# Two transformer blocks on one core: one weight group and spread modulation loads for one-stream feed-forwards, waits by halves for two streams, and matmuls of constants around the transposes

## The chip, the cores and the metric

The kernel runs on one core of a Trainium2 chip. The metric is the device time of one execution in microseconds (us), as the median of several runs. The core has TensorE (PE, matrix multiply), VectorE (DVE), ScalarE (ACT), GpSimd (POOL), and SyncE (SP), whose queue issues nearly all DMAs. They run their own instruction streams and meet only at semaphores.

## What is computed

Two blocks in float32 on 256 tokens of width 1024. Block 1 has two layers; each is feed-forward, mixer, feed-forward, and works on two streams, the tokens `x` and a context of the same size. The mixer of layer 0 is a gated MLP (gMLP), that of layer 1 is attention. After that attention only `x` goes on. Block 2 has two layers of feed-forward, mixer ("mix": attention, convolution and gated linear attention side by side), feed-forward, on `x` alone.

```python
def ffn_sublayer(x, shift, scale, gate, w_in, w_out, ln_g, ln_b):          # block 1
    y = swiglu(modulate(x, shift, scale), w_in, w_out)
    return layer_norm(ALPHA * x + 0.5 * gate * y, ln_g, ln_b)

for l in range(DEPTH):                                                      # block 2
    mod = c_act @ ada_w[l] + ada_b[l]
    sh1, sc1, gt1, sh2, sc2, gt2, sh3, sc3, gt3 = jnp.split(mod, N_MOD, axis=-1)
    h = _modulate(_rmsnorm(x, ffn1_norm[l]), sh1, sc1)
    x = x + FFN_RES * gt1[:, None, :] * _swiglu(h, ffn1_w_in[l], ffn1_w_out[l])
    ...                                                                     # mixer, second feed-forward
```

`swiglu(h, w_in, w_out)` is `(silu(h @ w_g) * (h @ w_u)) @ w_out` with an inner width of 2816, that is 22 chunks of 128. Every sublayer has its own shift, scale and gate vectors (three sections of 1024), each a product of a condition vector with a 1024 x 1024 matrix.

## The kernel before

**Stages.** `plan()` lists twelve stages, here called by their number: 0 feed-forward, 1 gMLP, 2 and 3 feed-forward, 4 attention (its input has two streams, its output one), 5 feed-forward, all block 1; 6 feed-forward, 7 mix, 8 and 9 feed-forward, 10 mix, 11 feed-forward, all block 2. Stages 0 to 4 have two streams (512 columns a matmul), 5 to 11 one (256). The feed-forwards with one stream are 5, 6, 8, 9 and 11.

**Units.** The weights come in units of 1 MB (two DMAs) through two slots of `wraw`. Each unit is split into a high part `wh` (ACT, L697) and a low part `wl` (DVE, L1023, function `split_next`), and every product is three matmuls (L1656). SP may load unit u when `wl` of unit u-2 is made (L428). ACT makes `wh` of a unit only when PE is through with the unit two before it (L696), and PE starts a unit when its `wl` is there.

**A feed-forward** goes in two groups, `GROUPS = (12, 10)` chunks of the inner width. For each group there is a features phase (one unit a chunk: gate and up products into the PSUM banks 0,1 or 2,3, then ACT's silu L758, DVE's product `ht` L1245, POOL's split into `hh` and `hl` L557, L558) and an out phase (one unit for two chunks, L1779). The y tiles of an out phase, 128 tokens by 1024, take two banks each: banks 0 to 7 with two streams, 4 to 7 with one. After each group `take_y` (DVE, L1114 and L1117) adds the gated tiles to `x`, and adds 1 to `y_evac` when the last tile has left PSUM. PE waits for `y_evac` before a group's features with two streams (L1838), and for `pair_free`, the last `ht`, before every out phase (L1841). In stages whose input isn't scaled yet, DVE multiplies and adds the layer norm's gain and bias to `x` after the features of the first group (`scale_x`, L1249, instructions of L1137), ahead of the split of the second out unit.

**The modulation of the next stage** is made during the features phase of the first group: 12 DMAs of 1 MB (`mraw`, L421) and for each of them two DVE operations a stream (`mod_unit`, L1000). Three sections of four pieces q go by turns of four units. `mods_taken` (L351) says that the first unit of a turn takes pieces 0 and 1, the second piece 2, the third piece 3. `mods_loaded` (L354) issues pieces 0 and 1 at unit 1 of SP's turn and 2 and 3 at unit 3. At a section's end PE turns the row into columns (`columns`, L1665) and DVE copies them (`mod_end`).

**Between two stages** PE runs `gate_rows` (L1676, f32 matmuls of `ones` with `acc` after `y_evac`), then `transposes` (L1696, 16 a stream, f32, `ident` moving) after the norm of the stage, which DVE, ACT and POOL make; ACT and DVE evacuate and split the transposed input (L728, L1083, L736, L1075), and then the next features start (L1710, or L1750 in mix and attention).

Of the kernel before, what the change touches and what calls it, by code (L numbers as in the profile page):

```python
# [6 lines left out]
P = 128  # L7
# [10 lines left out]
T = 256  # L18
# [4 lines left out]
GROUPS = (12, 10)  # L23
# [17 lines left out]
CW = 256  # L41

# [9 lines left out]
def plan():  # L52
# [14 lines left out]
    n = dict(unit=FIRST, inq=FIRST, h=FIRST, sg=0, group=0, pre=0, tr=0, mix=0, tile=0)  # L67
    for i, s in enumerate(subs):
# [6 lines left out]
        if s["kind"] == "ffn":  # L75
            n["unit"] += KF + KF // 2
# [3 lines left out]
            n["group"] += len(GROUPS)  # L80
            n["tile"] += len(GROUPS) * (TT * ns - 1)
        elif s["kind"] == "gmlp":
# [4 lines left out]
            n["group"] += 2  # L87
            n["tile"] += 2 * (TT * ns - 1)
# [68 lines left out]
def program(nc, ins, out, subs):  # L157
    u_end = subs[-1]["n_unit"] + dict(ffn=33, gmlp=36, attn=10, mix=16)[subs[-1]["kind"]]
    with ExitStack() as ctx:
# [76 lines left out]
        zt = (zt0, zt1)  # L236

# [62 lines left out]
        y_evac = sem("y_evac")  # L300
# [50 lines left out]
        def mods_taken(per, j, i):  # L351
            return [(i, q) for q in ((0, 1), (2,), (3,), ())[j]] if per == 4 else [(j // 2, 2 * (j % 2) + q) for q in (0, 1)]

        def mods_loaded(per, j, i):  # L354
            if per == 4:
                return [(i, q) for q in ((), (0, 1), (), (2, 3))[j]]
            n = j - 2 if j else 0
            return [] if j in (1, 2) else mods_taken(per, n, i)

        def section_done(per, j, i):  # L360

            sec = (i if j == per - 1 else None) if per == 4 else (j // 2 if j % 2 else None)
# [46 lines left out]
        def _(sp):  # L409
# [66 lines left out]
            for s in subs:  # L476
                nxt = after(s)
                if s["kind"] == "ffn":
# [4 lines left out]
                    for g, n in enumerate(GROUPS):  # L483

                        phase(n, 2 if g else 4, lambda idx: [
# [54 lines left out]
        def _(pool):  # L540
# [69 lines left out]
            for s in subs:  # L610
# [15 lines left out]
                if s["kind"] == "ffn":  # L626
                    m0 = 0
                    for g, n in enumerate(GROUPS):
# [59 lines left out]
        def _(act):  # L688
# [50 lines left out]
            for s in subs:  # L739
# [7 lines left out]
                if s["kind"] == "ffn":  # L747
                    W = T * len(s["streams"])
                    m0, u0 = 0, s["n_unit"]
                    for g, n in enumerate(GROUPS):  # L750
# [224 lines left out]
        def _(dve):  # L975
# [122 lines left out]
            def take_y(s, streams, bank0, u, first, tiles=None, by=zt):  # L1098
# [5 lines left out]
                for i in range(n):  # L1104
# [9 lines left out]
                    steps.link(dve.tensor_tensor(by[t][:], ps[:, b:b + 2].rearrange("p a b -> p (a b)"), gate[:, c], ALU.mult))  # L1114
                    if i == n - 1:
# [108 lines left out]
            for s in subs:  # L1224
# [8 lines left out]
                if s["kind"] == "ffn":  # L1233
                    W = T * len(s["streams"])
                    m0, u0 = 0, s["n_unit"]
                    for g, n in enumerate(GROUPS):
# [10 lines left out]
                        phase(n, u0, 2 if g else 4, evac, None if g else nxt)  # L1247
# [8 lines left out]
                        take_y(s, s["post"], 0 if W == 2 * T else 4, u0, g == 0, s["n_tile"] + g * (W // P - 1),  # L1256
                               zt if g else zm)
# [397 lines left out]
        def _(pe):  # L1655
# [23 lines left out]

            def transposes(s):  # L1680
# [86 lines left out]
            def out_unit(u, count, width, bank0, chunk0, ready, start=False, stop=False, halves=None):  # L1767
# [4 lines left out]
                for t in range(width // P):  # L1772
# [437 lines left out]
```

## Time and profile before

| | us |
|---|---|
| median of 3 runs | 3416.32 (3415.41 to 3417.49) |
| the profiled execution | 3414.92, of which the span of the trace is 3413.2 |
| PE busy / DVE busy / ACT busy / POOL busy in the span | 3116.1 / 2017.1 / 969.2 / 651.2 |
| TensorE clock granted, mean | 0.954 of full speed |
| DMA, mean | 153 GB/s |

All rows are of one execution. PEclk 1.00 is 2.4 GHz and 0.50 is 1.2 GHz. Matmuls overlap, so that the last of a run ends 0.2 to 0.4 us after its slot; the distance between starts is the rate. "DVEq" or "issue" as the end of a wait is an instruction of a queue (a semaphore) or one that the trace doesn't show.

### The profile page before, as it was taken

The page shows a single profiled execution, that of the slowest core. Times are in us where ns is not written, and L with a number is a line of the kernel's source. Part 1 is how long each engine was busy: PE and PEld are TensorE (multiplying, and loading weights), DVE is VectorE, ACT ScalarE, POOL GpSimd, SP SyncE. Part 2 cuts the span into 40 slices and gives each one's busy share as a digit, 9 for nine tenths or more (in the row PEclk, how much of TensorE's full clock was granted, in tenths as well). Part 3 has the DMA queues.
Part 4 walks back from the last instruction along what each step waited for, and adds up shares of the span by engine and source line. Part 5 has one row for each costly group of instructions (what it writes and reads, how often), then busy time and mean ns, then how long its engine had stood idle before and what let it go on. Part 6 is the DMA issues. An engine that isn't in the chain of part 4 may idle for free.

```text
span 3413.2 us, 45375 instructions
## 1 busy us (share of the span) xinstructions
PE 3116.1 (91%) x17444; PEld 2660.2 (78%) x17444; DVE 2017.1 (59%) x1834; ACT 969.2 (28%) x981; POOL 651.2 (19%) x628
## 2 busy tenths in 40 slices
PE   7999989999989999899988799799888989989799
PEld 3877779877768787777867689688877878978688
DVE  6653366656276434773348775664687557457654
ACT  1111222212122121211214333333533333343333
POOL 0110100214011010110100031122552103227011
PEclk9999989999989999899999899899889989989899
DMA  7533235222254333443333686675447658654355
GB/s 274 163 124 89 95 112 173 99 87 75 87 155 152 100 86 111 136 136 99 98 102 124 202 269 182 202 229 179 171 148 239 208 176 281 189 172 151 120 178 159
DMA packets 501022, 523.00 MB, mean 153 GB/s; under 512 B 15652, under 2 KB 432726, under 8 KB 500886
## 3 DMA queue, kind: packets, MB, share of 16 engines
q1 hardware_dynamic: 497720, 513.76, 46.8%
q0 software_dynamic: 3168, 7.36, 1.0%
q8 instruction: 96, 1.57, 0.2%
q14 instruction: 38, 0.31, 0.0%
HBM read 520.01 MB, written 1.05 MB: 153 GB/s over the span
## 4 chain that ended last, share of the span: by engine, by line
PE 70%; DVE 15%; issue 5%; DMA 4%; ACT 3%; POOL 2%; SPq 1%; DVEq 0%; ACTq 0%; POOLq 0%
PE ps L1710 37%; PE ps L1779 19%; PE ps L1750 7%; DMA mraw<-in_ada_w 3%; DVE wl L1023 3%; DVE acc L1000 2%; DVE x L1117 2%; ACT wh L697 2%; DVE x L1137 1%; PE ps L1696 1%; PE ps L1665 1%; DVE zt L1114 1%; POOL wst L667 1%; DVE mraw L1114 1%; ACT ptmp L728 1%
## 5 line engine op out<-in xcount | busy, mean ns | idle before, releaser
L1023 DVE TENSOR_TENSOR wl<-wraw,wh 128x2048 fp32r<-128x2048 f32 x341 | 846.9, 2484 | 681.6 <-ACT wh L697 672.7
L1710 PE MATMUL ps<-xh,wh 128*128 128x256 f32 (+1 forms) x3008 | 1003.4, 334 | 68.0 <-DVE xl L1075 38.2
L1710 PE MATMUL ps<-xh,wl 128*128 128x256 f32 (+1 forms) x3008 | 996.0, 331 | 0.0
L1710 PE MATMUL ps<-xl,wh 128*128 128x256 f32 (+1 forms) x3008 | 995.0, 331 | 0.0
L697 ACT ACTIVATE wh<-wraw 128x2048 fp32r<-128x2048 f32 x341 | 652.3, 1913 | 655.5 <-PE ps L1779 622.5
L1710 PEld LDWEIGHTS ps<-xh,wh 128*128 128x128 f32 x3008 | 574.7, 191 | 135.3 <-issue 65.0
L1710 PEld LDWEIGHTS ps<-xl,wh 128*128 128x128 f32 x3008 | 573.7, 191 | 58.8
L1710 PEld LDWEIGHTS ps<-xh,wl 128*128 128x128 f32 x3008 | 574.6, 191 | 57.5
L1000 DVE SCALAR_TENSOR_TENSOR acc<-mraw,svec,acc 128x1024 f32<-128x1024 f32 x329 | 431.6, 1335 | 44.4 <-DMA mraw<-in_ada_w 29.9
L557 POOL CAST hh<-ht 128x256 f32 (+1 forms) x176 | 135.7, 771 | 1578.3 <-DVE ht L1245 1578.3
L1779 PE MATMUL ps<-wh,hh 128*128 128x512 f32 x968 | 386.6, 399 | 25.5 <-DVE ht L1245 19.8
L1779 PE MATMUL ps<-wl,hh 128*128 128x512 f32 x968 | 384.9, 398 | 0.0
L1779 PE MATMUL ps<-wh,hl 128*128 128x512 f32 x968 | 384.5, 397 | 0.0
L758 ACT ACTIVATE sg<-ps 128x256 f32<-128x256 f32 (+1 forms) x176 | 81.8, 465 | 983.7 <-PE ps L1710 983.7
L1245 DVE TENSOR_TENSOR ht<-ps,sg 128x256 f32<-128x256 f32 (+1 forms) x176 | 92.0, 523 | 380.2 <-ACT sg L758 379.7
L1750 PE MATMUL ps<-wh,xh 128*128 128x256 f32 x896 | 265.0, 296 | 37.2 <-DVE wl L1023 19.1
L1750 PE MATMUL ps<-wl,xh 128*128 128x256 f32 x896 | 261.3, 292 | 0.0
L1750 PE MATMUL ps<-wh,xl 128*128 128x256 f32 x896 | 260.7, 291 | 0.0
L1779 PEld LDWEIGHTS ps<-wh,hh 128*128 128x128 f32 x968 | 182.9, 189 | 74.9 <-DVE ht L1245 24.4
L1779 PEld LDWEIGHTS ps<-wh,hl 128*128 128x128 f32 x968 | 183.1, 189 | 44.4
L1779 PEld LDWEIGHTS ps<-wl,hh 128*128 128x128 f32 x968 | 182.9, 189 | 43.7
L1750 PEld LDWEIGHTS ps<-wh,xh 128*128 128x128 f32 x896 | 179.2, 200 | 41.6 <-DVE wl L1023 21.9
(332 smaller groups left out, 2981.2 us busy)
## 6 DMA issues: line engine op xcount, KB each, us to landing
wraw<-in_ffn_w_in SPq DMA_DIRECT2D x352, 512.0 KB, 5.1
wraw<-in_ffn_w_out SPq DMA_DIRECT2D x176, 512.0 KB, 4.2
mraw<-in_ada_w SPq DMA_DIRECT2D x72, 1024.0 KB, 7.4
mraw<-in_w_mod SPq DMA_DIRECT2D x64, 1024.0 KB, 5.7
wraw<-in_gmlp_w_in SPq DMA_DIRECT2D x48, 512.0 KB, 4.5
wraw<-in_mix_w_in SPq DMA_DIRECT2D x48, 512.0 KB, 4.6
wraw<-in_gmlp_w_out SPq DMA_DIRECT2D x24, 512.0 KB, 4.3
first_w<-in_w_mod SPq DMA_DIRECT2D x8, 1024.0 KB, 13.4
```

The source lines that it names most:

```text
L557: steps.link(pool.tensor_copy(hh[:, where], ht[:, par, 0:width]))
L667: op = pool.tensor_scalar(term, ch_t[:, 1, tap:tap + T], cw_t[:, 1, tap:tap + 1], cw_t[:, 1, CONV_K:CONV_K + 1] if tap == 0 else None, ALU ...
L697: act.activation(wh[:, slot], wraw[:, slot], ACT.Copy).then_inc(whi_done, 1)
L758: act.activation(sg[:, pair, 0:W], ps[:, 2 * pair, 0:W], ACT.Silu).then_inc(sg_ready, 1)
L1000: op = dve.scalar_tensor_tensor(out=acc[:, c], in0=mraw[:, q % 2, jj], scalar=svec[:, v, 2 * q + jj:2 * q + jj + 1], in1=biasrow[:] if q = ...
L1023: dve.tensor_tensor(wl[:, slot], wraw[:, slot], wh[:, slot].bitcast(F32), ALU.subtract)\
L1114: steps.link(dve.tensor_tensor(by[t][:], ps[:, b:b + 2].rearrange("p a b -> p (a b)"), gate[:, c], ALU.mult))
L1117: last = steps.mark(dve.scalar_tensor_tensor(out=x[:, c, t], in0=x[:, c, t], scalar=ALPHA if first and s["block"] == 1 else 1.0, in1=by[t] ...
L1245: dve.tensor_tensor(ht[:, pair, 0:W], ps[:, 2 * pair + 1, 0:W], sg[:, pair, 0:W], ALU.mult)\
L1710: m = pe.matmul(ps[:, bank, 0:width], a, b, start=k == p == 0, stop=k == KD - 1 and p == 2)
L1750: m = pe.matmul(to, a, b, start=k == p == 0, stop=k == KD - 1 and p == 2)
L1779: m = pe.matmul(ps[:, bank0 + 2 * t + half], a, b, start=start and kk == p == 0, stop=stop and kk == 1 and p == 2, skip_group_check=not st ...
```

## The change

The feed-forwards with one stream have one group of 22 chunks, whose y tiles are taken once, with the unused second halves of `gate` and `acc` as temporaries. Their modulation goes by turns of eight units, one piece at a time; the last six units (two turns of eight fit in 22) take the four pieces of the last section by lists of their own. The out phase no longer waits for `pair_free` with one stream. With two streams and in the gMLP, `take_y` adds 1 to a new semaphore `y_half` after its second tile, on which the features phase (banks 0 to 3) now waits; the first out unit writes the tiles of banks 4 to 7 first and waits for `pair_free` before the others (in the gMLP the order stays, and the wait moves to the third tile). In all feed-forwards the split of the second out unit comes ahead of `scale_x`. In the gMLP DVE's order is as it was. `keep_going(bank, 16)` issues 16 f32 matmuls of `ones` with `ident`, 128 columns each, into a bank that nobody reads: ahead of the transposes of stages 1 to 11, and behind the transposes of stages 5 to 11.

```diff
-GROUPS = (12, 10)
+GROUPS = {2: (12, 10), 1: (22,)}
+LAST_TAKEN, LAST_LOADED = (0, 1, 3, 5), (0, 2, 4, 5)
...
+        by_one = (gate[:, 1], acc[:, 1])
...
         def mods_taken(per, j, i):
+            if per == 8:
+                at = LAST_TAKEN if isinstance(i, int) and i == 2 else (0, 2, 4, 6)
+                return [(i, q) for q in range(4) if at[q] == j]
...
         def mods_loaded(per, j, i):
+            if per == 8:
+                at = LAST_LOADED if isinstance(i, int) and i == 2 else (1, 3, 5, 7)
+                return [(i, q) for q in range(4) if at[q] == j]
...
@@ take_y
+                    if i == TT - 1 < n - 1:
+                        dve.sem_inc(y_half, 1)
...
@@ DVE, feed-forward
-                        phase(n, u0, 2 if g else 4, evac, None if g else nxt)
+                        phase(n, u0, 2 if g else 8 if one else 4, evac, None if g else nxt)
+                        split_next(u0 + n)
                         if g == 0:
                             scale_x(s, s["post"])
...
-                        phase(n // 2, u0 + n, 2)
+                        phase(n // 2 - 1, u0 + n + 1, 2)
...
@@ PE
+            def keep_going(bank, n):
+
+                for _ in range(n):
+                    pe.matmul(ps[:, bank, 0:P], ones[:], ident[:], start=True, stop=True)
...
-                for t in range(width // P):
+                for n, t in enumerate(late[0] if late else range(width // P)):
+                    if late and n == TT:
+                        late[1]()
...
                 gate_rows(s)
+                if s["i"]:
+                    keep_going(3, 16)
                 transposes(s)
+                if len(s["post"]) == 1 and len(s["streams"]) == 1:
+                    keep_going(7, 16)
...
-                            pe.wait_ge(y_evac, s["n_group"] + g)
-                        features_phase(n, u0, s["n_inq"] + m0, W, 2 if g else 4, None if g else nxt)
-
-                        pe.wait_ge(pair_free, s["n_inq"] + m0 + n + 1)
+                            pe.wait_ge(y_half, s["n_half"] + g)
+                        features_phase(n, u0, s["n_inq"] + m0, W, 2 if g else 4 if both else 8, None if g else nxt)
+
                         pe.wait_ge(y_evac, s["n_group"] + g)
...
-                                  lambda i: pe.wait_ge(h_ready, s["n_h"] + m0 + 2 * i + 3))
+                                  lambda i: pe.wait_ge(h_ready, s["n_h"] + m0 + 2 * i + 3),
+                                  late=((2, 3, 0, 1), lambda: pe.wait_ge(pair_free, s["n_inq"] + m0 + n + 1)) if both else None)
...
@@ PE, gMLP
-                        pe.wait_ge(y_evac, s["n_group"] + g)
+                        pe.wait_ge(y_half, s["n_half"] + g)
...
+                            if i == first:
+                                pe.wait_ge(y_evac, s["n_group"] + g)
...
-                        pe.wait_ge(pair_free, q1 + first + n + 1)
+                        pe.wait_ge(sg_ready, s["n_sg"] + 2 * (first + n))
...
+                                  late=((0, 1, 2, 3), lambda: pe.wait_ge(pair_free, q1 + first + n + 1)))
```

## Rows read from the trace of the kernel before

**Rows 1.** The page: busy time of each engine; the chain of waits by engine.

```profile
PE 3116.1 (91%) x17444; PEld 2660.2 (78%) x17444; DVE 2017.1 (59%) x1834; ACT 969.2 (28%) x981; POOL 651.2 (19%) x628
...
PE 70%; DVE 15%; issue 5%; DMA 4%; ACT 3%; POOL 2%; SPq 1%; DVEq 0%; ACTq 0%; POOLq 0%
```

**Rows 2.** PE's waits over the span: line, releaser, us in total, times, longest.

```profile
PE ps L1710 <- DVE xl L1075: 38.2, 8, 5.0
PE ps L1696 <- issue: 34.9, 6, 13.8
PE ps L1676 <- DVEq L1116: 31.5, 11, 7.8
...
PE ps L1710 <- DVE wl L1023: 21.2, 24, 2.0
PE ps L1779 <- DVE ht L1245: 19.8, 16, 1.6
...
PE ps L1710 <- DVEq L1116: 8.6, 4, 2.3
PE ps L1779 <- DVE wl L1023: 8.0, 5, 2.0
...
PE ps L1779 <- DVEq L1310: 7.3, 2, 3.7
```

**Rows 3.** The chain, first out phase of stage 8: start, us, what.

```profile
2668.21 28.27 PE ps L1779 x120
```

**Rows 4.** The chain, first out unit of stage 2: start, us, what.

```profile
1112.31 6.06 DVE x L1137 x4
...
1118.39 4.64 DVE x L1137 x4
...
1123.34 2.30 DVE wl L1023
...
1125.69 2.62 PE ps L1779 x7
```

**Rows 5.** The page's group of `mod_unit`: busy, mean ns | idle before.

```profile
L1000 DVE SCALAR_TENSOR_TENSOR acc<-mraw,svec,acc 128x1024 f32<-128x1024 f32 x329 | 431.6, 1335 | 44.4 <-DMA mraw<-in_ada_w 29.9
```

**Rows 6.** Stretches of stage 8: features of first and second group; busy, clock, DMA share, GB/s.

```profile
2590.00:2667.00 77.00, 73.66 (x606) 72.85 (x605) 64.62 (x50) 24.96 (x23) 27.19 (x21) 0.97 0.90 287
...
2703.00:2758.00 55.00, 54.38 (x466) 54.13 (x465) 29.32 (x22) 21.18 (x19) 10.23 (x18) 1.00 0.65 188
```

**Rows 7.** PE's timeline from stage 8's end into stage 9: start, us [idle before].

```profile
2791.20 2.69 PE L1676 MATMUL ps<-acc,ones 128*128 128x512 f32 x4 [2.77 <-DVEq L1116]
2797.28 3.65 PE L1696 MATMUL ps<-ident,z 128*128 128x128 f32 x16 [3.39 <-issue]
2805.65 0.58 PE L1710 MATMUL ps<-xh,wh 128*128 128x256 f32 x1 [4.72 <-DVE xl L1075]
```

**Rows 8.** Short stretches at the starts of stages 9 and 8; columns as in rows 6.

```profile
2788.90:2792.20 3.30, 0.99 (x3) 0.55 (x4) 3.15 (x3) 0.00 (x0) 0.00 (x0) 1.00 1.01 393
2792.30:2795.70 3.40, 1.59 (x3) 0.03 (x1) 0.42 (x3) 2.19 (x4) 0.72 (x1) 0.50 1.05 275
...
2580.70:2584.00 3.30, 3.30 (x16) 3.21 (x16) 0.00 (x0) 0.00 (x0) 0.00 (x0) 0.50 0.00 0
2584.10:2587.40 3.30, 0.16 (x2) 0.00 (x0) 1.90 (x4) 3.07 (x6) 0.00 (x0) 1.00 0.00 0
```

**Rows 9.** First features of stages 5 and 11, at 0.50 of the clock; columns as before.

```profile
1945.50:1949.10 3.60, 3.60 (x17) 3.60 (x18) 3.00 (x3) 2.49 (x2) 0.00 (x0) 0.50 0.00 0
...
3215.00:3218.90 3.90, 3.90 (x18) 3.90 (x19) 3.69 (x3) 1.04 (x1) 0.00 (x0) 0.50 0.02 4
```

**Rows 10.** PE's timeline in the gMLP: f32 matmuls of 128 columns at full clock.

```profile
641.73 0.38 PE L1877 MATMUL ps<-wst,ones 128*128 128x128 f32 x2
...
642.17 1.95 PE L1881 MATMUL ps<-wst,v 128*128 128x128 f32 x16
```

**Rows 11.** PE's timeline at the start of stage 1: transposes at full clock.

```profile
467.13 1.97 PE L1696 MATMUL ps<-ident,x 128*128 128x128 f32 x16 [1.32 <-DVEq L1159]
```

More of the change, by code:

```diff
@@ L65, in plan @@
             subs.append(dict(block=2, layer=l, kind=kind, part=part, streams=(0,), post=(0,)))
-    n = dict(unit=FIRST, inq=FIRST, h=FIRST, sg=0, group=0, pre=0, tr=0, mix=0, tile=0)
+    n = dict(unit=FIRST, inq=FIRST, h=FIRST, sg=0, group=0, half=0, pre=0, tr=0, mix=0, tile=0)
     for i, s in enumerate(subs):
@@ L75, in plan @@
         if s["kind"] == "ffn":
+            s["groups"] = GROUPS[ns]
             n["unit"] += KF + KF // 2
@@ L79, in plan @@
             n["sg"] += KF
-            n["group"] += len(GROUPS)
-            n["tile"] += len(GROUPS) * (TT * ns - 1)
+            n["group"] += len(s["groups"])
+            n["half"] += len(s["groups"]) if ns == 2 else 0
+            n["tile"] += len(s["groups"]) * (TT * ns - 1)
         elif s["kind"] == "gmlp":
@@ L87, in plan @@
             n["group"] += 2
+            n["half"] += 2
             n["tile"] += 2 * (TT * ns - 1)
@@ L482, in _ @@
                     m0 = 0
-                    for g, n in enumerate(GROUPS):
-                        phase(n, 2 if g else 4, lambda idx: [
+                    for g, n in enumerate(s["groups"]):
+                        phase(n, 2 if g else 4 if len(s["streams"]) == 2 else 8, lambda idx: [
                             w_in[:, :, t, bass.ds(idx + m0, 1), :].rearrange("p k m c -> p k (m c)")
@@ L627, in _ @@
                     m0 = 0
-                    for g, n in enumerate(GROUPS):
+                    for g, n in enumerate(s["groups"]):
                         pool.wait_ge(w_used, s["n_unit"] + 18 * g)
@@ L749, in _ @@
                     m0, u0 = 0, s["n_unit"]
-                    for g, n in enumerate(GROUPS):
+                    for g, n in enumerate(s["groups"]):
                         q0 = s["n_inq"] + m0
@@ L1235, in _ @@
                     m0, u0 = 0, s["n_unit"]
-                    for g, n in enumerate(GROUPS):
+                    one = len(s["groups"]) == 1
+                    for g, n in enumerate(s["groups"]):
                         q0, h0 = s["n_inq"] + m0, s["n_h"] + m0
@@ L1253, in _ @@
                             factors(nxt)
-                        phase(n // 2, u0 + n, 2)
+                        phase(n // 2 - 1, u0 + n + 1, 2)
                         u0 += n + n // 2
-                        take_y(s, s["post"], 0 if W == 2 * T else 4, u0, g == 0, s["n_tile"] + g * (W // P - 1),
-                               zt if g else zm)
+                        take_y(s, s["post"], 4 if one else 0, u0, g == 0, s["n_tile"] + g * (W // P - 1),
+                               by_one if one else zt if g else zm)
                         m0 += n
@@ L1765, in all_tokens_phase, with out_unit @@
                 mod_loop(pe, n, per, body, mods)
-            def out_unit(u, count, width, bank0, chunk0, ready, start=False, stop=False, halves=None):
+            def out_unit(u, count, width, bank0, chunk0, ready, start=False, stop=False, halves=None, late=None):
                 slot = u % 2
@@ L1783, in out_unit, with out_phase @@
                 m.then_inc(w_used, 1)
-            def out_phase(n, u0, width, bank0, ready, halves=None):
+            def out_phase(n, u0, width, bank0, ready, halves=None, late=None):
                 for i in range(n):
-                    out_unit(u0 + i, u0 + i, width, bank0, 2 * i, lambda: ready(i), i == 0, i == n - 1, halves)
+                    out_unit(u0 + i, u0 + i, width, bank0, 2 * i, lambda: ready(i), i == 0, i == n - 1, halves,
+                             None if i else late)
             def input_halves(chunk, t):
```

8 lines of the change are left out of this document (4 added, 4 removed).

## The prediction, as it went on record

> **What bounds the kernel now.** I read the page first: PE is busy for 91% of the span and holds 70% of the chain [rows 1]. So only three things count: time in which PE waits, time in which it works at half clock, and work put on it. The view of PE's waits sorts the first kind [rows 2]. The stretches of the trace with their granted clock give the second, and PE's timeline at the stage boundaries shows how much room there is for added matmuls; both are taken up below. All terms below are differences in PE's time, since next to nothing else is late at the end.
>
> **Waits that the finer order removes.**
> Start of an out phase: PE waits 19.8 us in all, 16 times, for the last `ht` [rows 2]. That is every group of the feed-forwards: six with two streams (about 1.5 each), ten with one (about 1.1). With one stream the y banks 4 to 7 are apart from the banks 0 to 3 that `ht` reads, and no wait is left. With two streams the first two tiles take banks 4 to 7: 24 matmuls at 0.236 us [rows 3] are 5.7 us of work ahead of a wait that would have been over in 1.5. The low half of the first out unit is made before the last `ht` in either order, so nothing else is late there. **19.8 off.** Five of these sixteen phase starts no longer exist at all, which comes to the same.
> Start of the second group's features with two streams, and in the gMLP: 8.6 us, four times, for the last of four tiles [rows 2]. `y_half` comes two tiles, so about 5 us, earlier, ahead of PE's end of the out phase. **8.6 off.**
> Start of an out phase in the gMLP: 7.3 us, twice [rows 2]. The new wait, for ACT's `sg`, is over before the gating matmuls end, and half an out unit (5.7 us) covers the 3.7. But in the first group DVE still does 12 us of `scale_x` before the second out unit's split, and PE waits for that already now; there the second unit starts when it did, and the gain is given back. **3.7 off, of 7.3.**
> `scale_x` [rows 4]: in stage 2 it takes 10.7 us, then `wl` 2.3, and the second out unit starts 13.4 us after the last `ht`, where the first out unit (48 matmuls) is 11.4 long: 1.9 lost, in stage 3 the same. With the split first, the 10.7 us lie beside two out units (22.4 us) with the next split: 1.9 off in each. In stage 5 it takes 5.3 (four of those eight operations) and an out unit 5.6: counted from the end of the features, `wl` of the second out unit is ready at 5.0, `scale_x` ends at 10.3, the next `wl` at 12.6, where PE wants it at 11.2. So 1.4 of the 2.0 come back one unit later. **4.4 off**, out of the 8.0 of five waits [rows 2]; the other two are not touched.
>
> **One group with one stream, modulation by eight.** PE waits 21.2 us, 24 times, for `wl` in the features phases [rows 2], all of them in feed-forwards with one stream, nearly all in the first groups of stages 5, 6, 8 and 9, where the modulation is made, the rest behind `take_y`. Why: a unit of features is 48 matmuls at 55 us / 466 [rows 6], so a split has to be ready 5.6 us after the one before it. In a turn's first unit DVE does two pieces, four operations of 1.3 us [rows 5], beside 2.3 for the split and 0.4 for `ht`: 8 us of work in 5.6. In the first group DVE is busy for 64.6 of 77 us and DMA for 0.90 of the time; in the second for 29.3 of 55 and 0.65 [rows 6]. Spread over 22 units (about 124 us): DVE 22 x 3.0 and the difference of 29, so 95 us or 0.77. DMA 0.65 x 5.6 = 3.64 us a unit; twelve units are 43.7 of the 69.3 seen, which leaves 25.6 us for the modulation; so 80.1 + 25.6 = 105.7 in 127, or 0.83, and 0.85 to 0.92 in the last six units, which take four pieces. A unit with one piece fits: split done at 5.0 us, piece at 7.6, `ht` at 8.0, and the next `wh` is not there before 8.3. SP issues a piece two units, some 11 us, before it is used. What could be left is lateness of DMA in the last six units, from 0 to 17. I keep 1 us a stage. **17 off.** The pieces moved on SP's queue go behind each weight unit's pair, so a unit's weights queue behind at most one piece, not two. The `take_y` that disappears is DVE time that PE only feels as part of these waits: nothing more.
>
> **The matmuls of constants, price.** An f32 matmul is two PE instructions in the trace (x2 for one call), and 16 of 128 columns take 1.95 us with 0.28 of tail: 0.111 us each [rows 10]. So a block of 16 is 32 x 0.111 = 3.6 us at full clock. Transposes in f32 take 1.97 for 16 at full clock [rows 11] and 3.65 at half [rows 7]; by their distances the block is 32 x 0.215 = 6.9 us at half clock. Eighteen blocks are 65 to 124 us, so it matters where they lie.
> Ahead of the transposes of stages 7 to 11, PE sits idle for 3.4 us in stage 9 [rows 7], up to 5.5 in the mixes; these waits and the longer one of stage 6 are the 34.9 us of [rows 2]. `gate_rows` in front of it took 2.7 us, part of it at half clock. So at full clock 3.6 us go in with about 0.5 to spare. Behind the transposes PE is idle for 4.7 us [rows 7], one of the eight waits of 38.2 us in all [rows 2]: 3.6 goes in with 1.1 to spare, 6.9 would be 2.2 late.
> With two streams (stages 1 to 4) the block delays the first stream's transposes by 0.5 to 4 us, but DVE is busy with the second stream's norm meanwhile and comes to them some 3.8 us later. Nothing; between 2 us of gain and 6 of loss for the four.
>
> **What the clock gives back.** In stage 9 the clock was full while PE did the last out unit and was idle for 2.8 us, and fell to half in the next stretch [rows 8]; it came back only in the features. All seven one-stream stages begin their features at 1.2 GHz, for 3.6 to 5.6 us, 29.9 in all (the first and the last are [rows 9]). At 2.4 GHz that work is half as long: 14.9. A run of 16 transposes at half clock was followed by full clock (from 2580.70 and from 2584.10) [rows 8], and they stream `ident`, as the new matmuls do, at the same 0.215 us; so I take it that these raise and hold it. The idle 2.8 us ahead of `gate_rows` stay, so it will often still fall once there and come back under the first block, which then ends up to 1 us late. I take nine tenths: **13.4 off**. The transposes of stages 7 to 11 run at full clock, 3.65 - 1.97 = 1.7 us less each, minus 0.6 each for the late block: **5.4 off**. In stages 5 and 6 the norm between is long or DVE late; transposes there stay at half clock and only the second block helps.
>
> The Trainium skill, "TensorE: Matmul & The Clock Gate", Part 4 (PE-mode transpose), says that the full clock doesn't engage for transposes, as they don't count as busy. The row disagrees: full clock followed right behind 3.6 us of nothing but transposes [rows 8].
>
> **Sum.** 19.8 + 8.6 + 3.7 + 4.4 + 17 + 13.4 + 5.4 = 72.3 us off the profiled execution's 3414.9, so 3342.6. The median of the runs is 1.4 above that execution: **3344.0**.
>
> **Rivals.**
> (a) The clock is held at only half of the boundaries, because the fall comes later than I think, between the blocks: half of 18.8 lost, 3353.4. For it: the idle time in front of `gate_rows` is unchanged. 0.13.
> (b) DMA is the next bound in the one-group phase: the 17 don't come, 3361. For it: 0.85 to 0.92 near the end of the phase, and 0.90 is where stalls are seen now [rows 6]; against it: DMA reached 393 GB/s between stages [rows 8], and 287 in the stalling phase. 0.10.
> (c) The two-stream waits are taken over by the next one (a split behind `take_y` or `scale_x`): half of 19.8 + 8.6 + 3.7 + 4.4, 3362. Against it: splits have 11.2 us a unit there. 0.03.
> (d) Transposes don't count for the clock: stages 5 and 6, where they come first after idle time, start their features at half clock and with the second block 2.2 us late: about 4.5 each, 3353. This is what the skill's Part 4 would make of it. 0.03.
> (e) The blocks never raise the clock, and run at half clock. Then they are late by 4.5 in stages 8, 9 and 11, 3.1 in the mixes, 4.2 in stage 5, 2.3 behind seven sets of transposes, 0.7 with two streams: 43. Only 53.5 - 43 = 10 off, 3406. 0.05.
> (f) **Slower:** the blocks lie on the path in full at half clock, 18 x 6.9 = 124 us against 53.5: 3487. That needs PE to come to them when the norm is already there, and it decides at 53.5 / 18 = 3.0 us a block. Against it: 3.4 and 4.7 us of measured idle time at both places [rows 7]. 0.04.
> My forecast has the remaining 0.62. Its own range is 3330 to 3355; with (a) to (d) 3328 to 3370, which leaves out (e), (f) and some of the tails. Within 0.2% (7 us, about what a measurement of this kernel can tell from no change) needs a mixture of (e) and (b): 0.01. Slower 0.04, faster 0.95.
>
> **What the profile after would show.** PE's waits for `ht` (L1245) ahead of the out phase gone, the waits for L1116 only ahead of `gate_rows`, those for `wl` in features a few us instead of 21; DVE's idle time for `mraw` small and, if (b), in the last six units. Mean clock up from 0.954 to about 0.965. The first 3.6 us of features in stages 5 to 11 at 1.00; if (a) or (e), 0.50. Transposes of 1.97 instead of 3.65 in stages 7 to 11. The forecast is wrong if the blocks' 32 instructions take far more than 3.6 us, if they end after the norm by more than a microsecond, or if `wl` is still late in the phase of 22 units.

## The result and the profile after

The changed kernel took **3322.4 us** (median of four runs, 3317.3 to 3327.0) beside 3415.9 for the kernel before in the same job; the ratio is 0.9728, 95% interval 0.9711 to 0.9745. A second set of five runs gave 0.9724 (0.9711 to 0.9738). The forecast of 3344 had the sign, and the mechanisms that it named were at work, but the time lies 6 us below the low end of its range. The profiled execution took 3321.9 with a span of 3320.1, so 93.1 us less than the 3413.2 before, where 72.3 had been forecast. Some 21 us of gain were not foreseen, and they are what the experiments are about.

The page of the changed kernel, busy time and the chain by engine (answers to [rows 1]):

```profile
PE 3137.9 (95%) x18020; PEld 2698.3 (81%) x18020; DVE 1988.0 (60%) x1814; ACT 972.5 (29%) x985; POOL 635.6 (19%) x628
...
PE 80%; DVE 10%; ACT 3%; POOL 3%; issue 2%; DMA 2%; SPq 0%; DVEq 0%; ACTq 0%; POOLq 0%
```

PE works longer than before (3137.9 against 3116.1), with the 18 x 32 = 576 instructions of the blocks in it, and still ends 93 us earlier.

PE's waits in the changed kernel (line, releaser: us in total, times, longest), to be held against [rows 2]:

```profile
PE ps L1691 <- DVEq L1129: 31.5, 11, 8.0
...
PE ps L1730 <- DVE xl L1086: 19.7, 8, 4.9
...
PE ps L1716 <- issue: 14.3, 5, 9.2
...
PE ps L1801 <- DVE wl L1034: 10.4, 4, 7.2
...
PE ps L1730 <- DVE wl L1034: 3.4, 7, 0.6
```

The lines have moved: L1691 is `gate_rows`, L1716 the transposes, L1730 the features, L1801 the out phase. The wait of the out phase for `ht` (19.8), that of the features for the y tiles (8.6) and that of the gMLP's out phases (7.3) have no row any more. The features' wait for `wl` fell from 21.2 to 3.4. The wait for `xl` ahead of the features and the one ahead of the transposes, 38.2 and 34.9 before, are halved, since the blocks lie in them. One row grew by more than 0.2 us: the out phase's wait for `wl`, from 8.0 to 10.4.

PE's timeline from stage 8's end into stage 9 (against [rows 7]):

```profile
2720.04 1.96 PE L1691 MATMUL ps<-acc,ones 128*128 128x512 f32 x4 [2.47 <-DVEq L1129]
2721.83 3.73 PE L1698 MATMUL ps<-ident,ones 128*128 128x128 f32 x32
2726.12 1.94 PE L1716 MATMUL ps<-ident,z 128*128 128x128 f32 x16 [0.56 <-issue]
2727.90 3.74 PE L1698 MATMUL ps<-ident,ones 128*128 128x128 f32 x32
2732.78 0.38 PE L1730 MATMUL ps<-xh,wh 128*128 128x256 f32 x1 [1.15 <-DVE xl L1086]
```

A block takes the forecast 3.6 us and its tail, and leaves 0.56 us ahead of the transposes and 1.15 behind them (0.5 and 1.1 were forecast). The transposes take 1.94 instead of 3.65. From `gate_rows` to the first feature it is 12.74 us, 14.45 before.

First features of stages 5 and 11 (against [rows 9]), and then two stretches of stage 8's one phase of 22 units (against [rows 6]): busy time, clock, DMA share, GB/s:

```profile
1909.90:1913.50 3.60, 3.57 (x30) 3.58 (x31) 3.00 (x3) 2.53 (x2) 0.00 (x0) 1.00 0.02 5
...
3127.90:3131.50 3.60, 3.58 (x30) 3.59 (x31) 3.39 (x3) 1.07 (x1) 0.00 (x0) 1.00 0.01 2
2528.00:2595.00 67.00, 66.98 (x571) 66.78 (x572) 47.64 (x38) 25.73 (x23) 18.09 (x22) 1.00 0.82 247
2595.00:2655.00 60.00, 59.93 (x514) 59.73 (x513) 41.95 (x32) 22.35 (x20) 17.42 (x21) 1.00 0.92 285
```

The first features run at full clock, with 30 matmuls in 3.6 us where there were 17. In the phase of 22 units PE is busy throughout, DVE for 0.71 and 0.70 of the time, and DMA at 0.92 near the end does not hold it up.

**Where the 93 us went.** I sorted the distances between the starts of successive matmuls, over the whole span, into work at full speed, the surplus of work done at half clock, and idle time. Before to after: work +63.9, surplus at half clock -32.0, idle -125.1, together -93.2. The blocks' own work, 18 x 3.57 = 64.3, is all the work that came, and it lies in idle time. Such a sorting depends on how it is done: with the median distance of each form at full clock as its work, the same two traces give +63.9, -30.1 and -127.0, so each part is known to some 2 to 4 us.

### The profile page after: what moved, and what is told of

Read it like the earlier page. It is cut to its first block, busy times and chain, and to the rows that moved or that the text cites. A ratio compares the mean times of both kernels' runs of the same rounds, so it can differ in the third digit from the quotient of the medians.

```text
span 3320.1 us, 45976 instructions
## 1 busy us (share of the span) xinstructions
PE 3137.9 (95%) x18020; PEld 2698.3 (81%) x18020; DVE 1988.0 (60%) x1814; ACT 972.5 (29%) x985; POOL 635.6 (19%) x628
## 4 chain that ended last, share of the span: by engine, by line
PE 80%; DVE 10%; ACT 3%; POOL 3%; issue 2%; DMA 2%; SPq 0%; DVEq 0%; ACTq 0%; POOLq 0%
PE ps L1730 43%; PE ps L1801 22%; PE ps L1770 7%; DVE wl L1034 2%; PE ps L1680 1%; ACT wh L708 1%; POOL wst L678 1%; PE ps L1716 1%; DVE x L1130 1%; PE ps L1833 1%; DMA wraw<-in_ffn_w_in 1%; POOL lnp L684 1%; ACT ptmp L739 1%; PE ps L1698 1%; DVE st L1157 1%
## 5 line engine op out<-in xcount | busy, mean ns | idle before, releaser
L1730 PE MATMUL ps<-xh,wh 128*128 128x256 f32 (+1 forms) x3008 | 994.3, 331 | 23.1 <-DVE xl L1086 19.7
L1730 PE MATMUL ps<-xl,wh 128*128 128x256 f32 (+1 forms) x3008 | 989.3, 329 | 0.0
L1730 PE MATMUL ps<-xh,wl 128*128 128x256 f32 (+1 forms) x3008 | 989.2, 329 | 0.0
L1730 PEld LDWEIGHTS ps<-xh,wh 128*128 128x128 f32 x3008 | 568.4, 189 | 84.7 <-issue 25.5
L1730 PEld LDWEIGHTS ps<-xl,wh 128*128 128x128 f32 x3008 | 568.0, 189 | 58.5
L1730 PEld LDWEIGHTS ps<-xh,wl 128*128 128x128 f32 x3008 | 568.3, 189 | 57.3
L1801 PE MATMUL ps<-wh,hh 128*128 128x512 f32 x968 | 383.2, 396 | 1.7 <-DVE wl L1034 1.7
L1801 PE MATMUL ps<-wh,hl 128*128 128x512 f32 x968 | 382.9, 396 | 0.0
L1801 PE MATMUL ps<-wl,hh 128*128 128x512 f32 x968 | 382.8, 395 | 0.0
L568 POOL CAST hh<-ht 128x256 f32 (+1 forms) x176 | 94.0, 534 | 1361.4 <-DVE ht L1259 1361.4
L569 POOL TENSOR_TENSOR hl<-ht,hh 128x256 f32 (+1 forms) x176 | 218.1, 1239 | 29.2 <-POOL hh L568 29.2
L1801 PEld LDWEIGHTS ps<-wh,hh 128*128 128x128 f32 x968 | 181.9, 188 | 46.6 <-DVE wl L1034 2.9
L1801 PEld LDWEIGHTS ps<-wh,hl 128*128 128x128 f32 x968 | 181.9, 188 | 44.0
L1801 PEld LDWEIGHTS ps<-wl,hh 128*128 128x128 f32 x968 | 181.9, 188 | 43.6
## 6 DMA issues: line engine op xcount, KB each, us to landing
first_w<-in_w_mod SPq DMA_DIRECT2D x8, 1024.0 KB, 13.4
```

Source lines behind the costliest of these rows:

```text
L568: steps.link(pool.tensor_copy(hh[:, where], ht[:, par, 0:width]))
L569: pool.tensor_tensor(hl[:, where], ht[:, par, 0:width], hh[:, where].bitcast(F32), ALU.subtract)\
L1730: m = pe.matmul(ps[:, bank, 0:width], a, b, start=k == p == 0, stop=k == KD - 1 and p == 2)
L1801: m = pe.matmul(ps[:, bank0 + 2 * t + half], a, b, start=start and kk == p == 0, stop=stop and kk == 1 and p == 2, skip_group_check=not st ...
```

## The experiments

**The blocks out, and the blocks alone.** The first kernel is the changed one without its two calls of `keep_going`; the second is the kernel before with these calls.

```diff
 gate_rows(s)
-if s["i"]:
-    keep_going(3, 16)
 transposes(s)
-if len(s["post"]) == 1 and len(s["streams"]) == 1:
-    keep_going(7, 16)
```

> The changed kernel without its 18 blocks of constant matmuls; everything else as in it. The whole change took 93 us off where 72 were forecast. Theory of the record (structure 53.5, blocks 18.8): this kernel is 53 to 56 us faster than the kernel before, about 3361, and its blocks are worth some 38 (then the missing 20 lie in what the blocks do to the clock). Rival A (the structure was sized too low, because every removed wait inside a stage had also let the clock fall, and the first dense work behind it ran at 1.2 GHz): 70 to 75 us faster, about 3343, blocks worth 20.

> The kernel before with the 18 blocks alone (16 f32 matmuls of constants ahead of the transposes of stages 1 to 11 and behind those of stages 5 to 11). Forecast for this part: 18.8 us faster, about 3397. If the blocks did more for the clock than I sized, 25 to 38 faster, first features at full clock in all of stages 5 to 11 and less time at 1.2 GHz in stages 1 to 4 as well. If they only work together with the structure (fewer waits later), under 12.

Without the blocks: 3342.4 us, ratio 0.9791 (0.9770 to 0.9812), so the finer waits and the one group bring **71 us, not 53.5**. The blocks alone: 3398.6, ratio 0.9957 (0.9942 to 0.9972), so 15 us; on top of the rest they bring 20 in the medians (21 by the ratios, with some 9 us either way; 18.8 forecast). Most of the error is in the structure, then. PE's waits without the blocks:

```profile
PE ps L1730 <- DVE xl L1086: 38.0, 8, 4.9
...
PE ps L1801 <- DVE wl L1034: 13.0, 6, 7.1
...
PE ps L1730 <- DVE wl L1034: 4.2, 8, 0.9
```

All rows of PE's waits summed: 289.9 us in 118 waits before, 241.2 in 80 here. That is 48.7 less, close to the 53.5 of the sum. The waits that were to go went, and little took their place: the out phase's wait for `wl` is 13.0 where 8.0 was, 7.1 of it in the gMLP and three of 1.33 us in stages 5, 6 and 9. But the span fell by 72.5: work -1.8, surplus at half clock -12.2, idle -58.9. So two things are missing in a sum of wait rows: 10.2 us of idle time that no row counts, and 12.2 us of clock. (The other way of sorting gives work 0, surplus -10.2, idle -62.6: 10 to 14 us beyond the rows, and 10 to 12 of clock.) The 70 to 75 us of the rival theory came true, but its reason, the clock, is only a part of the missing 19.

In the kernel before with blocks, the features' wait for `wl` grew from 21.2 to 27.2: at full clock PE takes up a split sooner than DVE makes it, and part of the blocks' gain is lost there. With one group it isn't (4.2 without blocks, 3.4 with them). In the profiles the blocks alone bring 15.0 us and on top of the rest 20.6, and these 6 us are the difference; the intervals of the runs are too wide to tell 15 from 20.

```profile
PE ps L1715 <- DVE wl L1023: 27.2, 29, 2.5
```

**What a wait costs beyond its row.** PE's timeline at the start of an out phase, in the kernel before (stage 8, first group) and in the changed one:

```profile
2666.92 0.28 PE L1710 MATMUL ps<-xl,wh 128*128 128x256 f32 x1
2668.21 0.50 PE L1779 MATMUL ps<-wh,hh 128*128 128x512 f32 x1 [1.01 <-DVE ht L1245]
2668.55 0.39 PE L1779 MATMUL ps<-wl,hh 128*128 128x512 f32 x1
```

```profile
2655.69 0.28 PE L1730 MATMUL ps<-xl,wh 128*128 128x256 f32 x1
2655.81 0.40 PE L1801 MATMUL ps<-wh,hh 128*128 128x512 f32 x1
2656.04 0.40 PE L1801 MATMUL ps<-wl,hh 128*128 128x512 f32 x1
```

The row says 1.01 us of idle time. But back to back the next matmul starts 0.12 after the start of this one, and with the wait it is 1.29: the 0.16 us by which a matmul is longer than its turn are normally hidden under the next, and a wait lays them bare. And the first matmul after the wait has its successor 0.34 later, not 0.23 as in the second timeline. So this wait costs 1.01 + 0.16 + 0.11 = 1.28. With 38 waits fewer, 38 x 0.27 = 10.3, beside the 10.2 (by the other sorting 14) that no row counts. The one wait is typical: over 60 waits between such matmuls at full clock in the kernel before, the medians of the two parts are 0.16 and 0.10 us, the means 0.17 and 0.13.

The 0.16 could have been known. The Trainium skill, "TensorE: Matmul & The Clock Gate", Part 2, "Single matmul latency", gives a lone bf16 matmul at full clock (398 + N) / 2.4 ns for N columns, so 166 ns above its columns' time. The trace agrees, for these types too: 0.28 - 0.12 = 0.16 and 0.40 - 0.23 = 0.17.

**The two halves of the structure.** `one_group` keeps, of the changed kernel, the one phase of 22 units, the modulation by eight and the split ahead of `scale_x` with one stream; the waits with two streams and in the gMLP are those of before, and there are no blocks. `two_streams` is the counterpart: the feed-forwards with one stream are as before (two groups, the modulation by four, the wait for `pair_free`, the split behind `scale_x`), and what concerns two streams and the gMLP is as in the changed kernel.

```diff
 # one_group, against the changed kernel without blocks
-pe.wait_ge(y_half, s["n_half"] + g)
+pe.wait_ge(y_evac, s["n_group"] + g)
...
+if both:
+    pe.wait_ge(pair_free, s["n_inq"] + m0 + n + 1)
...
-split_next(u0 + n)
+if one:
+    split_next(u0 + n)
 # two_streams, against the same
-GROUPS = {2: (12, 10), 1: (22,)}
+GROUPS = {2: (12, 10), 1: (12, 10)}
...
+if not both:
+    pe.wait_ge(pair_free, s["n_inq"] + m0 + n + 1)
```

> Of the changed kernel only the part for one stream: one group of 22 units, modulation by eight, no wait for the last ht, in stage 5 the split ahead of scale_x. No blocks, two-stream stages as before. By the record: ten waits of 1.1 (11), 17 of 21.2 for wl, 0.6 of scale_x: 28.6 us faster, about 3387. Rival A adds the clock's falls behind these waits: 32 to 38 faster.

> Of the changed kernel only the part for two streams and the gMLP: waits by halves and the split ahead of scale_x in stages 0, 2 and 3. No blocks, one-stream stages as before. By the record: 8.8 + 8.6 + 3.7 + 3.8 = 24.9 us faster, about 3391. Rival A: two waits of 1.9 us behind scale_x were each followed by 3.4 us at 1.2 GHz, which adds 1.7 twice, and 28 to 35 faster.

`one_group` took 3374.8, ratio 0.9880 (0.9859 to 0.9901), so 41 us; `two_streams` 3373.1, ratio 0.9892 (0.9871 to 0.9912), so 37. Both are over their forecasts by some 12, and over the rival's ranges (32 to 38 and 28 to 35) as well. Their rows of waits, though, fell by just what was forecast: 28.9 us for one group (28.6) and 24.9 for two streams (24.9). By distances the idle time fell by 36.4 with 31 waits fewer (28.9 + 31 x 0.27 = 37.3) and by 29.6 with 17 fewer (24.9 + 4.6 = 29.5). So the surcharge per wait fits in three kernels (the other sorting gives 36.7 and 31.1). The surplus at half clock went up by 4.5 in the one profile and down by 12.5 in the other; in `two_streams` that is where the rest of its gain lies. `one_group`'s profile is of the slowest of its four runs, 33 us below the kernel before and not 41, so it doesn't show where the other 8 us lie. The two add up to 78, with intervals of 7 on each, against 71 for both together.

**The split ahead of `scale_x`.** The changed kernel, with the split of the second out unit behind `scale_x` again, in stages 2, 3 and 5:

```diff
-split_next(u0 + n)
+behind = g == 0 and unscaled(s)
+if not behind:
+    split_next(u0 + n)
 if g == 0:
     scale_x(s, s["post"])
 ...
+if behind:
+    split_next(u0 + n)
```

> The changed kernel with one order put back: in stages 2, 3 and 5 the split of the second out unit stands behind scale_x again. PE then arrives at the second out unit 3.5 us too early in stages 2 and 3 and 3.3 in stage 5 (of which 1.2 came back one unit later anyway). Accounting of the record (a wait costs its own length): 9 us slower than the changed kernel. Theory now (the clock falls to 1.2 GHz for 3.4 us behind each such wait, in which dense work loses 1.7): 14 us slower, and the trace shows a fall behind each of the three.

It took 3335.5, ratio 0.9778 (0.9762 to 0.9794), so by the ratios 17 us more than the changed kernel (18 beside its second set), where 9 were expected by wait alone and 14 with the clock. Stages 2, 3 and 5 are longer by 8.3, 6.3 and 4.3; stage 7, which the edit doesn't touch, is 6.7 shorter in this profile, so that the spans differ by 13.4 only. The sum had 4.4 for this edit. Half of the difference is a wait: the out phase's wait for `wl` is 19.6 us in total here, 10.4 in the changed kernel. That is 9.2, not 4.4, since with the wait for `ht` gone the first out unit starts a microsecond or more earlier, and what DVE has to do ahead of the second doesn't. The two edits need each other: the one alone would be given back in the other's place. The chain of waits over the start of stage 2's out phase, in this kernel and then in the changed one:

```profile
1099.47 0.69 DVE ht L1259
1100.16 6.06 DVE x L1150 x4
...
1106.25 4.64 DVE x L1150 x4
...
1111.02 2.30 DVE wl L1034
...
1113.37 11.83 PE ps L1805 x43
```

```profile
1089.89 6.07 PE ps L1730 x26
1095.95 29.17 PE ps L1801 x125
```

The other half is the clock. Stretches just behind the `scale_x` wait of stage 2: in the kernel before (the wait, and what follows), with the split behind again, and a stretch of the same out phase in the changed kernel, where the clock doesn't fall at all:

```profile
1123.10:1126.50 3.40, 1.54 (x8) 0.92 (x7) 2.99 (x2) 1.91 (x1) 1.13 (x2) 1.00 0.48 181
1126.60:1130.00 3.40, 3.40 (x10) 2.63 (x9) 1.50 (x1) 0.00 (x0) 0.00 (x0) 0.50 0.94 266
```

```profile
1114.90:1118.20 3.30, 3.30 (x9) 2.63 (x8) 0.61 (x1) 0.00 (x0) 0.00 (x0) 0.50 0.97 288
```

```profile
1116.40:1119.80 3.40, 3.40 (x16) 2.75 (x15) 0.00 (x0) 1.41 (x1) 0.00 (x0) 1.00 0.82 308
```

In the kernel before the wait of 1.86 us lies in the first stretch, at full clock; then the clock is at 1.2 GHz for 3.4 us, with PE busy all the time: 10 matmuls instead of 16. The same fall stands behind the same wait in stages 3 and 5, and one more behind a 2.0 us wait for `wl` in stage 6. It is there in `blocks_only` (stages 2, 3, 5) and `one_group` (2, 3), again in this kernel (3.4 us at half clock in stages 2 and 3, 6.8 in stage 5, so 6.8 us lost), and not where the split comes first. In the kernel before each is 3.4 us at half clock, so 1.7 us lost: 6.8 for the four. That is a little over half of the 12.2 us of clock; the rest is scattered, and see below for how much that can be. Not every such wait has a fall behind it: of the 13 waits of 1.5 to 2.3 us inside features and out phases of the kernel before, these four had one within 1 us, and the other nine (2.26 us at 1183.5, for one) had none.

**The gMLP.** In its first group the out phase's second unit waits for a split that stands behind 12 us of `scale_x`. PE's waits there, before (680 to 720 us) and after (676 to 716):

```profile
PE ps L1779 <- DVEq L1310: 3.7, 1, 3.7
PE ps L1779 <- DVE wl L1023: 0.7, 1, 0.7
```

```profile
PE ps L1801 <- DVE wl L1034: 7.2, 1, 7.2
```

The 3.7 that went came back as a longer wait, and more, because before the first out unit had run at half clock for a time and so hid some of DVE's lateness. The cure is the one of stages 2, 3 and 5:

```diff
+                        split_next(u1)
+                        u1 += 1
 ...
-                        for i in range(n):
+                        for i in range(n - 1):
```

> The changed kernel, and in the gMLP too the split of the second out unit ahead of scale_x, where PE now waits 7.2 us and works 6.8 us at 1.2 GHz behind it. If the wait alone counts: 7.4 us faster than the changed kernel. With the clock behind it: 9 to 11 faster.

It took **3310.3**, ratio 0.9696 (0.9681 to 0.9711): by the ratios 10 to 11 us below the changed kernel, as expected with the clock (9 to 11), and a version that beats both. The wait of 7.2 is gone, and so is the fall of the clock behind it (6.8 us at 1.2 GHz from 691.9, 3.4 lost). In its profile stage 1 is only 6.6 us shorter, since the clock is at half for 6.8 us more elsewhere in it (526.1 to 529.5, and 6.8 us instead of 3.4 at 573.9).

**Which blocks do the work.** `ahead_only` is the changed kernel without the blocks behind the transposes, `behind_only` without those ahead of them.

> The changed kernel without the seven blocks behind the transposes of stages 5 to 11; the eleven ahead stay. If the blocks ahead carry the clock through the 4.7 us of idle time behind the transposes as well, it is as fast as the changed kernel. My theory: the clock falls in those 4.7 us, features start at 1.2 GHz for 3.4 to 5 us in most of stages 5 to 11, so 9 to 13 slower; what stays is 1.2 to 1.7 a boundary from the faster transposes.

> The changed kernel without the eleven blocks ahead of the transposes; the seven behind stay. My theory: transposes of stages 7 to 11 at 1.2 GHz again (1.7 each, 8 us), the block behind them follows on them and brings the clock back within some 5 us, mostly before the features start, but is up to 2 us late: 8 to 14 slower than the changed kernel. If the two kinds of blocks only work together, 18 to 20 slower, as without any.

Ahead only: 3339.2, ratio 0.9772 (0.9753 to 0.9792), 15 us slower than with both, as expected up to 2 us. Behind only: 3325.6, ratio 0.9741 (0.9726 to 0.9756), only 4 to 6 us slower, with overlapping intervals, where 8 to 14 were expected. Stage 9 shows why. With the blocks ahead only (timeline, then the first features' stretch):

```profile
2738.54 1.94 PE L1716 MATMUL ps<-ident,z 128*128 128x128 f32 x16 [0.56 <-issue]
2745.20 0.58 PE L1730 MATMUL ps<-xh,wh 128*128 128x256 f32 x1 [4.72 <-DVE xl L1086]
```

```profile
2745.30:2748.90 3.60, 3.60 (x17) 3.60 (x18) 3.39 (x3) 0.98 (x1) 0.00 (x0) 0.50 0.00 0
```

With those behind only:

```profile
2726.90 3.60 PE L1716 MATMUL ps<-ident,z 128*128 128x128 f32 x16 [4.14 <-issue]
2730.29 3.78 PE L1698 MATMUL ps<-ident,ones 128*128 128x128 f32 x32
2735.23 0.38 PE L1730 MATMUL ps<-xh,wh 128*128 128x256 f32 x1 [1.15 <-DVE xl L1086]
```

```profile
2735.40:2739.00 3.60, 3.60 (x32) 3.60 (x33) 3.39 (x3) 0.92 (x1) 0.00 (x0) 1.00 0.00 0
```

Ahead only, the transposes are short, but the clock falls in the 4.72 us behind them. Behind only, the transposes are at half clock again (3.60), and the clock is full from 2730.4 on, right at their end; the block fills the idle time from there to the features. In the other six stages with one stream full clock is there up to 2.3 us after the transposes' end, inside the block, and ahead of the features. The block's worth doesn't hang on the block ahead, and what the block ahead brings is the transposes' 1.7 us in stages 7 to 11. Part of that is lost again in the mix stages: stages 7 and 10 of the changed kernel are only 1.9 and 3.2 us shorter than before, though their starts are shorter by 1.6 and 1.7.

`one_stream_blocks` has the blocks ahead only from stage 5 on, and `after_again` is the changed kernel itself, beside it on the same chip.

```diff
-if s["i"]:
+if s["i"] > 4:
     keep_going(3, 16)
```

> The changed kernel itself once more, so that the three versions sent with it can be set against it on the same chip. Its ratio to the kernel before was 0.9728; both theories expect 0.972 to 0.975 here, that is 3317 to 3330 us beside 3415.

> The changed kernel, with the blocks ahead of the transposes only in stages 5 to 11; stages 1 to 4 lose theirs. Theory A (the blocks do their work where one stream runs: in stages 1 to 4 the features begin at 1.2 GHz with the block too, for 3.9 to 5.2 us, so the block there changes no clock that lasts): within 3 us of the changed kernel, transposes of stages 1 to 4 perhaps 1 us longer. Theory B (the block shortens the transposes and so lets the DVE's work on them begin earlier): 1.7 us for each set of transposes that goes cold, up to 4 x 1.7 = 7 us slower. The run with no block ahead at all was about 4 us slower in all, which leaves at most that for these four if the other seven are worth nothing.

3320.7 and 3322.8, ratios 0.9724 (0.9711 to 0.9738) and 0.9721 (0.9708 to 0.9735). The four blocks of stages 1 to 4 bring and cost nothing that these runs can tell (intervals of 5 us on each), as the first theory had it.

**Blocks twice as long.**

```diff
-keep_going(3, 16)
+keep_going(3, 32)
 ...
-keep_going(7, 16)
+keep_going(7, 32)
```

> The changed kernel with blocks of 32 matmuls instead of 16. Eighteen further blocks of 3.57 us at full clock are 64 us of work more. Theory A (the idle time is used up by the first 16: of the 3.4 us ahead and 4.7 us behind that the kernel before had, 0.5 and 1.1 are left, so a further 3.6 us is late by 3.1 ahead in stages 8, 9 and 11 and by 2.5 behind in seven): 3 x 3.1 + 7 x 2.5 = 27 us slower, 3349, less the clock that it may gain in stages 5 and 6. Theory B (what counts is still the clock, 193 us at 1.2 GHz are left, and longer blocks hold it further): no slower than 3322. In stages 1 to 4, where the next work waits for DVE, neither expects more than 2 us a stage.

3355.1, ratio 0.9817 (0.9800 to 0.9833): 32 us slower than the changed kernel by the ratios, where the first theory had 27. Stage 9's start:

```profile
2744.48 1.96 PE L1691 MATMUL ps<-acc,ones 128*128 128x512 f32 x4 [2.46 <-DVEq L1129]
2746.27 7.31 PE L1698 MATMUL ps<-ident,ones 128*128 128x128 f32 x64
...
2755.16 7.31 PE L1698 MATMUL ps<-ident,ones 128*128 128x128 f32 x64
2762.23 0.36 PE L1730 MATMUL ps<-xh,wh 128*128 128x256 f32 x1
```

No idle time is left at either place, and from `gate_rows` to the features it is 17.75 us instead of 12.74. The idle time of [rows 7] was the right measure of what a block may take; for the mixes and stages 5 and 6 the expectation had 2.5 us each, and up to their features they are 3.4 to 5.5 longer.

**More blocks.** `gmlp_split`, with ten matmuls of constants ahead of the wait before `gate_rows`, and 24 and 16 behind the attention stage's two sets of transposes:

```diff
 pe.wait_ge(mod_used, 12 * s["i"] + 14)
+if s["i"]:
+    ...
+    keep_going(0 if both else 5 if kind == "attn" else 3, 10)
 pe.wait_ge(y_evac, s["n_group"])
 ...
 transpose_stream(src)
+if s["kind"] == "attn":
+    keep_going(7, 24 if k == 0 else 16)
```

> The version with the split first in the gMLP too (3310.3 us), with matmuls of constants at two more places: ten of them (2.2 us at full clock) ahead of the wait that precedes the gate rows, in eleven stages, where PE is idle for 2.8 us and the clock falls in most stages; and 24 and 16 behind the two transposes of the attention stage, whose features begin at 1.2 GHz. Theory A (the clock falls because PE idles there, and filling that time holds it): time at 1.2 GHz goes from 187 to about 140 us, gate rows of 1.2 us where they were 2.7 in some stages, 8 to 15 us faster, 3297 to 3302. Theory B (what is gained between two stages is taken back by the wait for the norm, which ends when DVE is ready, not PE): gate rows and transposes get shorter but the features start no earlier, 0 to 3 us faster. Slower by up to 5 if the ten end after the last of the y tiles.

**3306.8**, ratio 0.9681 (0.9668 to 0.9695), the lowest of all; by the ratios 5 us below `gmlp_split`, with overlapping intervals. PE's timeline at stage 8's end:

```profile
2702.11 2.39 PE L1705 MATMUL ps<-ident,ones 128*128 128x128 f32 x20
2704.66 1.98 PE L1698 MATMUL ps<-acc,ones 128*128 128x512 f32 x4 [0.15 <-DVEq L1129]
...
2710.84 1.94 PE L1725 MATMUL ps<-ident,z 128*128 128x128 f32 x16 [0.63 <-issue]
...
2717.50 0.38 PE L1739 MATMUL ps<-xh,wh 128*128 128x256 f32 x1 [1.15 <-DVE xl L1086]
```

The idle time ahead of `gate_rows` is filled, and PE's time at 1.2 GHz went from 201 to 161 us in the profiles. But from `gate_rows` to the features it is 12.8 us here, 13.7 in `gmlp_split`, whose gate rows ran at half clock (3.53 us long), and 12.7 in the changed kernel, whose didn't: the fill is worth 0.8 a stage, and only where the clock would have fallen. The attention stage became 4.0 us shorter. The second theory was nearer. That the norm on DVE sets the time between two stages fits these times, but no run here shortened the norm.

## Why the prediction was right or wrong

- **Start of the out phase, 19.8; second group's features, 8.6.** Right: both rows are gone. What was mis-sized is the price of a wait: 1.28 us for a row of 1.01. Over 38 waits that is 10.3 us, which the sum put at nothing: the first part of the missing gain.
- **gMLP, 3.7 of 7.3.** Right in kind, as the gain of the first group was given back to the split behind `scale_x`. 6.5 were given back (0.7 to 7.2), not 3.7. Moving that split recovers 10 to 11.
- **`scale_x`, 4.4.** Right in the rows: the out phase's waits for `wl` outside the gMLP's out phases went from 7.3 to 3.2, with 1.1 of stage 5's coming back one unit later (1.4 forecast). What the term lacked is the clock: three falls of 3.4 us, 5.1 lost. Put back in the changed kernel the edit costs more, 17 to 18, because with the wait for `ht` gone the wait is 9.2: this order also keeps what the first term gained.
- **One group, 17.** Right to a tenth in the rows: 21.2 to 4.2 without blocks. DMA is at 0.92 near the end and doesn't hold PE up, so rival (b) is out. So is (c): but for the gMLP's, only waits of 0.6 and 1.1 us came up (1.33 without blocks).
- **The clock as a term of the blocks only.** This is the step that failed, together with the price of a wait above. The prediction had a clock term of 18.8 for the blocks and none for the waits that the structure removes. Removing a wait of 1.9 us inside a phase also removes the fall that followed it. 6.8 us of this are tied to four places, 12.2 (10.2 by the other sorting) is the difference in the profile without blocks.
- **The blocks, 18.8.** Right: 20 on top of the rest, price 3.6, slack 0.5 and 1.1, all seven first features at full clock. Rivals (a), (d), (e) and (f) are out. Their division came out as well: 13.4 for the features and 15 lost without the blocks behind, 5.4 for the transposes and 4 to 6 lost without those ahead. What was not foreseen is that those behind do without those ahead. The premise that transposes raise the clock rested on one good row: of the seven sets in the one-stream stages of the kernel before, all at half clock, two (stages 7 and 8) had full clock at their end and five did not.
- **The sum.** 48.7 of rows, 10.2 beyond the rows, 12.2 of clock and 1.8 of work (the same instructions, so that the sorting's own error shows here) are 72.9 for the structure (72.5 in the spans), and 20.6 more for the blocks: 93.1. The range (3328 to 3370) was made only of doubts that cost time, save for the tails of single terms; none of its cases had the forecast gains as too small.

What stays open: 5.4 of the 12.2 us of clock aren't tied to any wait. The changed kernel's own two profiles differ by 8.4 us, 3320.1 and 3311.7, with 193 and 179 us at 1.2 GHz; 4 to 6 of it is surplus at half clock. A difference of this size can be chance in one profile. The medians of the runs (71 us without blocks) say that it isn't all chance, but not where it lies. Falls also stand at the matmuls of one column (`columns`, 22 times in a run): at 7 of the 22 in the kernel before, at 7 and at 5 in the changed kernel's two profiles, and partly at other places.

## What to carry to other kernels

A wait's row is the least that it costs: add the matmul's tail and the slow start behind it (0.27 us here), and look at the clock in the stretch that follows each wait. Cost the edits of a change one upon the other, not each against the kernel before, because a wait that is removed can make the next one longer. Filler matmuls are free up to the idle time that is there, and cost their full length beyond it; the place that counts is right ahead of the long phase, and what is ahead of a wait for another engine brings little.

## What the hardware showed that was not expected

- A wait of 1.86 us was followed by 3.4 us at 1.2 GHz, though PE was busy before it and after it (stretches above). I had looked for falls only at stage boundaries, with 2.8 us and more. Four of thirteen such waits had this fall, so the length alone doesn't decide it.
- The clock can rise with nothing but transposes ahead of it, or almost nothing. Stage 6 of the changed kernel: the last 5.6 of 9.2 us of idle time, the transposes, and 3 us of the block behind them.

```profile
2118.80:2124.40 5.60, 0.00 (x0) 0.00 (x0) 2.58 (x5) 2.19 (x4) 0.72 (x1) 0.50 0.00 0
2124.50:2128.10 3.60, 3.58 (x17) 3.60 (x18) 0.00 (x0) 0.00 (x0) 0.00 (x0) 0.50 0.01 2
2129.00:2132.00 3.00, 3.00 (x29) 2.97 (x27) 1.77 (x4) 2.97 (x5) 0.00 (x0) 1.00 0.00 0
```

  PE's timeline has the block from 2127.97 on, so full clock was there 1.0 us after its first matmul, with 3.6 us of transposes before that. The Trainium skill, "TensorE: Matmul & The Clock Gate", Part 4, has transposes not counting as busy; this row speaks against it, as [rows 8] did. With no block behind, in `ahead_only`, the same 3.65 us of transposes in stage 6 were followed by 4.73 us of idle time and features at 0.50. The clock there was at half from 2123.0 to 2143.5, so it didn't rise behind these transposes at all: they are followed by full clock at some places and not at others.
